# A third group of heads between scores and values in every attention, and the second block's gates as half of 1 + tanh(x/2)

## What is computed

```python
y_a = _gqa_axial(...)       # 8 query heads, 2 key heads, rotated
y_b = _diff_attention(...)  # 8 heads, two softmaxes each: p1 - lambda * p2
y_c = _mla(...)             # 8 heads from a normed latent of width 384 + 256
gates  = sigmoid(gate_logits.reshape(b, s, 3, d))
merged = sum_n(gates[n] * (y[n] @ w_branch[n]))
x = x + merged @ w_out
```

## Time and profile before

| | us |
|---|---|
| median of 3 runs | 2878.91 |
| lowest and highest | 2878.01, 2881.4 |
| the profiled execution | 2877.92 |
| its span, first to last instruction | 2876.1 |
| PE busy | 2621.8 (91% of the span) |
| DVE busy | 1857.5 (65%) |
| ACT busy | 1528.5 (53%) |
| granted TensorE clock, mean | 0.947 of full |

### The profile page before, as it was taken

How to read it: one execution, slowest core, us unless ns; L and a number is a source line. 1 busy time by engine, 2 the same in 40 slices (tenths; PEclk the granted TensorE clock), 3 DMA queues, 4 the chain that set the end, 5 groups by cost and what they waited for, 6 DMA issues and landing times.

```text
span 2876.1 us, 38647 instructions
## 1 busy us (share of the span) xinstructions
PE 2621.8 (91%) x16826; PEld 2333.3 (81%) x16826; DVE 1857.5 (65%) x1580; ACT 1528.5 (53%) x1466; POOL 0.2 (0%) x4
## 2 busy tenths in 40 slices
PE   6879999887999999999999997978799989878998
PEld 6769998776787877878787786877689988768998
DVE  5645445564688888888888884454565554546554
ACT  5244434432677767777776774455344444644443
POOL 0000000000000000000000000000000000000000
PEclk9879999987999999999999998999899999889999
DMA  5214554221599999989999894323145533223452
GB/s 202 90 58 147 183 185 158 100 79 59 193 366 349 365 350 361 354 348 362 348 365 351 349 364 158 118 88 132 54 152 191 189 134 118 82 95 114 151 191 88
DMA packets 83099, 585.32 MB, mean 204 GB/s; under 512 B 9480, under 2 KB 11208, under 8 KB 12272
## 3 DMA queue, kind: packets, MB, share of 16 engines
q1 hardware_dynamic: 82928, 582.81, 54.2%
HBM read 581.73 MB, written 1.05 MB: 203 GB/s over the span
## 4 chain that ended last, share of the span: by engine, by line
PE 82%; DVE 10%; ACT 6%; issue 1%; DMA 0%; ACTq 0%; SPq 0%; DVEq 0%
PE PS L1370 80%; ACT whi L500 2%; DVE wlo L842 2%; ACT pb L563 2%; PE PS L1754 1%; ACT pt L579 1%; PE PS L1516 1%; DVE hT L859 1%; DVE stat L937 1%; DVE pb L945 1%; DVE small L855 1%; DVE hT L910 0%; DVE pb L931 0%; DVE qe L1003 0%; DVE ke L1002 0%
## 5 line engine op out<-in xcount | busy, mean ns | idle before, releaser
L842 DVE TENSOR_TENSOR wlo<-raw,whi 128x2048 fp32r<-128x2048 f32 x550 | 1259.5, 2291 | 567.2 <-ACT whi L500 557.1
L500 ACT ACTIVATE whi<-raw 128x2048 fp32r<-128x2048 f32 x550 | 1052.0, 1913 | 375.4 <-PE PS L1370 375.3
L1370 PE MATMUL PS<-hhi,whi 128*128 128x256 f32 x1952 | 573.1, 294 | 31.9 <-DVE hlo L865 19.0
L1370 PE MATMUL PS<-hlo,whi 128*128 128x256 f32 x1952 | 563.9, 289 | 0.0
L1370 PE MATMUL PS<-hhi,wlo 128*128 128x256 f32 x1952 | 562.9, 288 | 0.0
L1370 PEld LDWEIGHTS PS<-hhi,whi 128*128 128x128 f32 x1952 | 385.7, 198 | 46.5 <-issue 40.6
L1370 PEld LDWEIGHTS PS<-hlo,whi 128*128 128x128 f32 x1952 | 386.6, 198 | 0.6 <-issue 0.5
L1370 PEld LDWEIGHTS PS<-hhi,wlo 128*128 128x128 f32 x1952 | 385.7, 198 | 0.0
L1370 PE MATMUL PS<-whi,xghi 128*128 128x512 f32 x896 | 360.0, 402 | 2.1 <-ACT pm L667 2.1
L1370 PE MATMUL PS<-whi,xglo 128*128 128x512 f32 x896 | 355.2, 396 | 0.0
L1370 PE MATMUL PS<-wlo,xghi 128*128 128x512 f32 x896 | 355.0, 396 | 0.0
(11 more groups left out here) (331 smaller groups left out, 3757.3 us busy)
## 6 DMA issues: line engine op xcount, KB each, us to landing
raw<-in_wm SPq DMA_DIRECT2D x336, 1024.0 KB, 5.0
raw<-in_ws SPq DMA_DIRECT2D x214, 1024.0 KB, 4.8
xT<-in_xT SPq DMA_DIRECT2D x1, 1024.0 KB, 4.9
bsum<-in_bsum SPq DMA_DIRECT2D x1, 1024.0 KB
out_T<-hT SPq DMA_DIRECT2D x4, 256.0 KB, 2.5
lmask<-in_lmask SPq DMA_DIRECT2D x1, 512.0 KB
tri<-in_tri SPq DMA_DIRECT2D x1, 256.0 KB
cmask<-in_cmask SPq DMA_DIRECT2D x1, 256.0 KB
```

What stands on the lines that cost most here:

```text
L500: act.activation(whi[s % SPLIT][:], raw[s % RAW][:], ACT.Copy).then_inc(hi_ready, 1)
L842: dve.tensor_tensor(wlo[s % SPLIT][:], raw[s % RAW][:], whi[s % SPLIT][:].bitcast(F32), ALU.subtract).then_inc(lo_ready, 1)
L1370: return pe.matmul(out, a, b, start=start, stop=stop, skip_group_check=True)
```

## The change

Three things are edited together.

1. In all attentions the stagger grows by one job. Each step n of after is

```diff
-            return out + [Projection(pair(sg, i), func=ACT.Sigmoid) for i in range(12)]
+            return out + [Projection(pair(sg, i), func=ACT.Tanh, scale=0.5) for i in range(12)]
...
-                for n in range(len(jobs) + 2):
+                for n in range(len(jobs) + 3):
...
-                    if n >= 2 and jobs[n - 2].value:
+                    if n >= 3 and jobs[n - 3].value:
                         after(mixed)
-                        act.activation(jobs[n - 2].dst, PS[:, 6, 0:2 * P].rearrange("p (t q) -> p t q", t=2),
+                        act.activation(jobs[n - 3].dst, PS[:, 6, 0:2 * P].rearrange("p (t q) -> p t q", t=2),
                                        ACT.Copy).then_inc(mixed_out, 1)
...
-                    if 1 <= n <= len(jobs) and jobs[n - 1].value:
-                        kb = jobs[n - 1].keys // P
+                    if 2 <= n <= len(jobs) + 1 and jobs[n - 2].value:
+                        kb = jobs[n - 2].keys // P
...
-                                       mg[:, 4 * jj + 2 * i:4 * jj + 2 * i + 2, :], ACT.Copy).then_inc(merged_hi, 1)
+                                       mg[:, 4 * jj + 2 * i:4 * jj + 2 * i + 2, :], ACT.Copy,
+                                       scale=0.5).then_inc(merged_hi, 1)
...
-                    if n < len(jobs):
+                    if 1 <= n <= len(jobs):
+                        j, pb = jobs[n - 1], pbs[(n - 1) % PB]
+                        z = stat[:, (n - 1) % PB, 4:8]
                         after(exped)
                         step(dve.reciprocal(z, z))
...
-                            first = pbs[(n - 1) % PB]
+                            first = pbs[(n - 2) % PB]
...
-                            dve.tensor_tensor(dst if n == 0 else gs[i][:], pair(sg, 4 * n + 2 * jj + i),
-                                              PS[:, b + i, :], ALU.mult).then_inc(gated, 1)
+                            dve.scalar_tensor_tensor(out=dst if n == 0 else gs[i][:], in0=pair(sg, 4 * n + 2 * jj + i),
+                                                     scalar=1.0, in1=PS[:, b + i, :], op0=ALU.add,
+                                                     op1=ALU.mult).then_inc(gated, 1)
...
-                        dve.tensor_tensor(mlo[:, ts, :], mg[:, ts, :], mhi[:, ts, :].bitcast(F32),
-                                          ALU.subtract).then_inc(merged_ready, 1)
+                        dve.scalar_tensor_tensor(out=mlo[:, ts, :], in0=mg[:, ts, :], scalar=0.5,
+                                                 in1=mhi[:, ts, :].bitcast(F32), op0=ALU.mult,
+                                                 op1=ALU.subtract).then_inc(merged_ready, 1)
...
-                    if n >= 2 and jobs[n - 2].value:
-                        j, pt = jobs[n - 2], pts[weighs % 2]
+                    if n >= 3 and jobs[n - 3].value:
+                        j, pt = jobs[n - 3], pts[weighs % 2]
...
-                        buf = pbs[(n - 1 - (j.less is not None)) % PB]
+                        buf = pbs[(n - 2 - (j.less is not None)) % PB]
...
-                        pe.wait_ge(probs_ready, before + n)
+                        pe.wait_ge(probs_ready, before + n - 1)
```

More of the change, by code:

```diff
@@ L923, in attention @@
                         sp = PS[:, b:b + 2, :].rearrange("p b (h k) -> p b h k", h=2)
-                        m, z = stat[:, n % PB, 0:4], stat[:, n % PB, 4:8]
+                        m = stat[:, n % PB, 0:4]
                         after(scored)
@@ L944, in attention @@
                         for i in range(4):
-                            ins = dve.tensor_scalar(pb[:, i, 0:w], pb[:, i, 0:w], z[:, i:i + 1], None, ALU.mult)
+                            w = slice(0, j.keys)
+                            ins = dve.tensor_scalar(pb[:, i, w], pb[:, i, w], z[:, i:i + 1], None, ALU.mult)
                         if j.less is not None:
                             step(ins)
-                            first = pbs[(n - 1) % PB]
+                            first = pbs[(n - 2) % PB]
                             ins = dve.scalar_tensor_tensor(out=first[:], in0=pb[:], scalar=j.less, in1=first[:],
@@ L1507, in attention @@
                         fill()
-                    if 1 <= n <= len(jobs) and jobs[n - 1].value:
-                        j = jobs[n - 1]
-                        buf = pbs[(n - 1 - (j.less is not None)) % PB]
+                    if 2 <= n <= len(jobs) + 1 and jobs[n - 2].value:
+                        j = jobs[n - 2]
+                        buf = pbs[(n - 2 - (j.less is not None)) % PB]
                         tp = banks(4, 2).rearrange("p (h b q) -> p h b q", h=4, b=NT)
                         claim(4, 2)
-                        pe.wait_ge(probs_ready, before + n)
+                        pe.wait_ge(probs_ready, before + n - 1)
                         for i in range(4):
```

## The result

The changed kernel takes 2898.69 us (median of 4 runs, 2896.14 to 2900.61) against 2880.15 of the kernel before on the same chip: ratio 1.0066, 95% interval 1.0051 to 1.0080. It is slower by 19 us. Its profiled execution took 2896.14 us with a span of 2894.3, 18.2 more than before.

A forecast was written before the change was run, and what follows sets the result against it. PE was taken to bound the kernel (82% of the chain), with ACT and DVE counting only where PE waits. Twice the per-layer terms gave 21.5 us, fox 1, together +22.5 on 2877.92: 2901 us, range 2882 to 2915.

The forecast's parts named there:

- The bare head norm, +9 per layer: Latent's head norm (cc): left without its two fillers, it costs +9 us per layer, from +6 to +11.
- Axial, +1.3: Axial attention: one more wait of 1.2 us for P, +1.3 us per layer, bounds +1.2 and +2.0.
- The sixth filler of diff, +0.8: Last step of diff: the added filler makes the next one wait for its drain, +0.8 us per layer, bounds 0 and +0.8.
- Diff, 0: Attention diff: shorter loop, longer start and PE waits that keep the clock falling, net 0 us per layer, from -3.3 to +2.
- Once the stagger is longer this order is gone (next step), so I take 0: Diff: P no longer stands behind whi, a table load and the drain, so removing loads gains 0 us.
- my bound of 2.6: Diff: removing table loads gains at most 2.6 us per layer, 1.3 at each of two waits for P.
- My walk through the longer stagger: Diff: summed instruction times, 25 us to M(1), two loops of 13.3, last interval 10.4, together 62.0 us.
- Latent, -0.5: Attention latent: shorter walk, mostly taken back by PE at half clock, -0.5 us per layer, from -2.8 to +1.
- Fox, +0.5 per layer: First block's attention: waits for P become others of about the same sum, one more of 1.2; +0.5 us, -1.2 to +1.5.
- Merge, +0.15: Merge stage: fused DVE products cost slightly more per column than plain ones, +0.15 us per layer, bounds 0 and +0.3.
- Rival 1: Diff: waits at T(1) and M(1) and the half clock behind them vanish, -16 us per layer, 2868 in all; chance 0.06.
- Rival 2: ACT's table switches: all 24 loads at 1.28 us are on the path, so -31 us, 2869 in all; chance 0.04.

The follow-up runs named there:

- the gates alone: The kernel before with its sigmoid gates computed as half of 1 + tanh(x/2) and nothing else changed: 2870.78 us, ratio 0.9967.

## Why the prediction was right, and where its steps were not

It said 2901 us (2882 to 2915), slower. Measured were 2898.69. It added 22.5 us to 2877.92; against the kernel before on the same chip the change is 18.5.

- **The bare head norm, +9 per layer.** Right: +8.9 in the stretches. Both tests name it as the cause: without it the change is no loss, and it alone costs as much as the change. All of its steps came, the wait for the square (2.7), the one for rs_lo (3.1), and the half clock (0.57 over the stretch, sums in 4.43 us where they took 2.3):

```profile
1991.46 4.43 PE L1376 MATMUL PS<-hT,selC 128*16 128x256 f32 x10 [2.73 <-ACT hT L536]
```

  Counting the fillers one by one through the whole mixer was the step that found it. Nothing in the stretch itself was edited.
- **Axial, +1.3.** Right within 0.3: one wait of 1.2 more, and a short one at M(0). In after three waits of 1.2 stand among the four.
- **The sixth filler of diff, +0.8.** Right: the way to the spread of y grew by 0.7.
- **Diff, 0.** The net was right (+0.7), its make-up wrong. The step that failed is "Once the stagger is longer this order is gone (next step), so I take 0" for the table loads. With one wait ahead of the exponential it holds: the load runs under it. It does not hold from step 4 on, where E has two waits and the one for the maximum stands ahead of the load. The gates gave 3.05 us per layer with the short stagger and 3.0 and 4.8 with the long one, above my bound of 2.6. With the two waits swapped the same loads cost nothing under the long stagger (67.1 us with sigmoid gates). Under the short one the trace shows the same two loads held, at 1.28 us each; there the swap was not tried. That these two come to 2.6, like my bound, is luck: I had priced the loads between whi and P. Against it stands the long stagger by itself, which costs 3.7 and 5.6 us with sigmoid gates. In the change the two cancel. My walk through the longer stagger (62.0 to M(7), and 65 with the 3 us given back) was short too: M(7) starts 66.2 us in, with M(1) at 26.2 where I had 25, and M(3) 15.1 behind it where I had 13.3. By their own terms the loop and the last interval add up to 13.2 and 10.3, 0.1 less each than I wrote. I also left out what a shorter wait saves in clock.
- **Latent, -0.5.** A term of the wrong size: -3.4, and I had named over 3 as a sign of being wrong, so here the prediction failed by its own test. The 20.5 and 23.3 us of its walk stand without their terms. I expected PE at half clock to take the gain back. The granted clock rose from 0.78 to 0.90 instead, and PE's busy time for the same 128 matmuls fell from 21.30 to 18.18 us. Those 3.1 us are nearly the whole gain. PE's waits within the stretch hardly changed in sum (6.5 us before, 6.2 after). My lower bound was -2.8, which left out that the clock itself might be better than before. Why it was better is not shown.
- **Fox, +0.5 per layer.** Too small: +1.9 and +3.0 in the stretches, +4.3 for both by the run that has it alone. N(0) fell behind the convolution as foreseen, T(0) came 7 us later and waited 4.9 us. The waits for P shrank only from 9.8 to 6.2, so PE waited 1.3 us more in the first layer, and it was busy 0.8 us longer, at a clock of 0.71 where it was 0.74.
- **Merge, +0.15.** The rows say 0. The fused product takes 686 ns where the plain one took 685 (groups on DVE, 2050 to 2110 us before and 2062 to 2125 after, columns as in the earlier trace rows):

```profile
L1285 DVE TENSOR_TENSOR mg<-sg,PS 128x512 f32<-128x512 f32 x4 | 2.7, 685 | 3.8 <-PE PS L1370 3.8
...
L1289 DVE SCALAR_TENSOR_TENSOR mg<-sg,PS 128x512 f32<-128x512 f32 x4 | 2.7, 686 | 3.6 <-PE PS L1376 3.5
```

  My two prices per column came from other tiles.
- **Projections from the latent.** They had no term and took 0.5 us less.

The errors of latent (-2.9 per layer), fox (+1.9 per layer) and the small ones have different signs, which is why the total came within 3 us. That closeness is luck; the direction and the largest term are not. Rival 1, the waits of diff vanishing, did not come true in the change, but its condition can be met in part: with the filler in odd steps the loop no longer has whi and wlo between E and N, the wait at T(1) is gone, and diff falls by 10 us below before, not by the rival's 16, since 4.2 us stay at M(1). Rival 2, every load on the path, is ruled out by the gates alone: 9.5 us, not 31.

The version that beats both is the one with the filler of diff in odd steps, at a ratio of 0.9908.

## What to carry to other kernels

Where independent work is dealt out from one list to fill waits, as here, an extra step in one place takes it from another. Count the list to its end, before and after, and look at the stage that comes out empty. When you deepen a stagger, look for what stands long in program order between a result and the engine that needs it. Here the deeper stagger paid in latent, which has no fillers, and in diff only once the filler had moved to the step in which its split does not precede the N that a T waits for. And where an instruction has two waits and a table load ahead of it, look at which of them stands ahead of the load, and write them so that it is the one satisfied early.

## What the runs showed of the hardware that I had not expected

A table load can hide under a wait or be held by it, as the order of two lines in the source has it. With one wait at the exponential the load ran ahead of it (1908.36); with two, the one written second stood ahead of the load, and when that was the maximum, the load began only after 1.78 us of idling (1937.38). Swapping the two lines moved diff from 70.31 and 72.07 us to 67.09 and 67.03. In the kernel before the order is the same and two loads per layer are held (1928.14); swapping it there, or together with the filler in odd steps, was not tried.

The same 128 matmuls of latent took PE 21.30 us in one kernel and 18.18 in another, at a granted clock of 0.78 and 0.90, though PE waited almost as long in both. In before the clock falls again behind a wait of 2.4 us for P, the longest there, and the last 6.9 us run at 0.75. In after no wait between the first scores and the last M is over 1.7 us, and the last 18 us run at full clock:

```profile
2045.00:2051.90 6.90, 4.51 (x40) 3.60 (x40) 1.21 (x5) 2.45 (x4) 0.00 (x0) 0.75 0.01 2
...
2058.00:2064.00 6.00, 3.59 (x44) 2.78 (x42) 0.00 (x0) 2.43 (x3) 0.00 (x0) 1.00 0.00 0
```

So in a stage with short bursts of PE work, what the edit did to the clock was worth nearly all of its 3.4 us.
